# The first column group of a large block kernel, reordered: each weight column serves both token halves in turn, filler matmuls in the gap, filter tables ahead of token rows, Hyena side work 8 tiles later

## The reference, cut to what matters

```python
hn = rmsnorm(x, norm1_w)                       # x: 256 x 2048
proj = hn @ w_in                               # the first product of the kernel
conv_out = centred_depthwise_conv(proj[..., :5120], conv_w, conv_b)
filt = hyena_filters(L, w1, b1, f1, w2, b2, f2, w3)   # two sine layers, then w3
z   = hx1 * long_conv(hv, kf[:, 0], hb[0])
y_a = hx2 * long_conv(z,  kf[:, 1], hb[1])
```

## Time and profile before

| what | value |
|---|---|
| median of 3 runs | 2603.71 us (2602.76 to 2605.73) |
| profiled execution, its own time | 2605.0 us |
| its span | 2603.2 us |
| PE busy | 2592.2 us of the span |
| ACT, POOL, DVE busy | 1407.6, 1208.0, 1129.5 us |
| HBM over the span | 188 GB/s |

### The profile page before, as it was taken

How to read it: one execution, slowest core, us unless ns; L and a number is a source line. 1 busy time by engine, 2 the same in 40 slices (tenths; PEclk the granted TensorE clock), 3 DMA queues, 4 the chain that set the end, 5 groups by cost and what they waited for, 6 DMA issues and landing times.

```text
span 2603.2 us, 30124 instructions
## 1 busy us (share of the span) xinstructions
PE 2592.2 (100%) x11856; PEld 2146.5 (82%) x11856; DVE 1129.5 (43%) x1324; ACT 1407.6 (54%) x1727; POOL 1208.0 (46%) x528
## 2 busy tenths in 40 slices
PE   9999999999999999999999999999999999999999
PEld 7888888788888888888888888888888888888887
DVE  5898955434442232323333466456533232322222
ACT  7677654445565555555544575565555555555333
POOL 2777843344444444444444455333444444444443
PEclk9999999999999999999999999999999999999999
DMA  8776654466666666666666644554566666666554
GB/s 298 220 201 205 193 186 162 147 233 210 202 196 211 204 205 205 205 207 202 209 207 210 212 162 162 173 184 146 178 203 204 208 202 210 202 210 202 202 202 146
DMA packets 174588, 515.84 MB, mean 198 GB/s; under 512 B 108027, under 2 KB 111068, under 8 KB 117104
## 3 DMA queue, kind: packets, MB, share of 16 engines
q1 hardware_dynamic: 174016, 513.40, 61.3%
q10 hardware_dynamic: 432, 0.52, 0.1%
HBM read 487.14 MB, written 2.10 MB: 188 GB/s over the span
## 4 chain that ended last, share of the span: by engine, by line
PE 94%; DVE 2%; DMA 1%; ACT 1%; POOL 1%; issue 1%; SPq 0%; ACTq 0%; DVEq 0%; POOLq 0%
PE PB L735 30%; PE PB L739 30%; PE PB L736 30%; DMA RAW<-in_w_in_a 1%; DVE WL L2011 1%; PE PB L971 1%; PE PB L815 0%; PE PB L933 0%; PE PB L753 0%; PE PB L855 0%; PE PB L845 0%; ACT WH L1256 0%; POOL WL L2967 0%; PE PB L1088 0%; PE PB L1028 0%
## 5 line engine op out<-in xcount | busy, mean ns | idle before, releaser
L2967 POOL TENSOR_TENSOR WL<-RAW,WH 128x1024 fp32r<-128x1024 f32 x441 | 1086.8, 2465 | 1378.0 <-ACT WH L1256 1377.7
L1256 ACT ACTIVATE WH<-RAW 128x1024 fp32r<-128x1024 f32 x889 | 938.8, 1058 | 1070.0 <-PE PB L739 1061.0
L2011 DVE TENSOR_TENSOR WL<-RAW,WH 128x1024 fp32r<-128x1024 f32 x448 | 614.7, 1373 | 1380.9 <-ACT WH L1256 1380.7
L735 PE MATMUL PB<-WH,HNH 128*128 128x512 f32 x2464 | 970.5, 394 | 2.2 <-ACT WH L1544 1.9
L739 PE MATMUL PB<-WL,HNH 128*128 128x512 f32 x2464 | 960.9, 390 | 2.1 <-POOL WL L2967 2.0
L736 PE MATMUL PB<-WH,HNL 128*128 128x512 f32 x2464 | 960.1, 390 | 0.0
L735 PEld LDWEIGHTS PB<-WH,HNH 128*128 128x128 f32 x2464 | 463.2, 188 | 102.2 <-issue 7.4
L739 PEld LDWEIGHTS PB<-WL,HNH 128*128 128x128 f32 x2464 | 463.0, 188 | 102.1 <-POOL WL L2967 4.3
L736 PEld LDWEIGHTS PB<-WH,HNL 128*128 128x128 f32 x2464 | 463.4, 188 | 94.3
L735 PE MATMUL PB<-WH,HDH 128*128 128x512 f32 x704 | 273.9, 389 | 0.0
L736 PE MATMUL PB<-WH,HDL 128*128 128x512 f32 x704 | 273.9, 389 | 0.0
(11 more groups left out here) (376 smaller groups left out, 1926.3 us busy)
## 6 DMA issues: line engine op xcount, KB each, us to landing
RAW<-in_w_gu SPq DMA_DIRECT2D x176, 1024.0 KB, 4.8
RAW<-in_w_dn SPq DMA_DIRECT2D x88, 1024.0 KB, 4.8
RAW<-in_w_in_a SPq DMA_DIRECT2D x53, 1024.0 KB, 5.3
RAW<-in_w_in SPq DMA_DIRECT2D x45, 1024.0 KB, 4.8
RAW<-in_w_out SPq DMA_DIRECT2D x32, 1024.0 KB, 4.8
RAW<-in_w_ga SPq DMA_DIRECT2D x24, 1024.0 KB, 4.7
RAW<-in_w_gb SPq DMA_DIRECT2D x24, 1024.0 KB, 4.8
WIN<-in_win SPq DMA_DIRECT2D x8, 512.0 KB, 6.5
```

Source lines behind the costliest of these rows:

```text
L735: e.matmul(o, hi[:, k, x], WH[:, s, c], start=k == 0, stop=False)
L1256: e.activation(WH[:, u % NSPL, :], RAW[:, n % NRAW, half * SU * 128:(half + 1) * SU * 128], ACT.Copy).then_inc(*wt.act.mark(("wh", u)))
L2011: e.tensor_tensor(WL[:, u % NSPL, :], RAW[:, n % NRAW, half * SU * 128:(half + 1) * SU * 128], f32(WH[:, u % NSPL, :]), ALU.subtract).then ...
L2967: e.tensor_tensor(WL[:, u % NSPL, :], RAW[:, n % NRAW, half * SU * 128:(half + 1) * SU * 128], f32(WH[:, u % NSPL, :]), ALU.subtract).then ...
```

## The change

Eight edits, all in the first part of the kernel:

1. Ahead of group 0, 11 ONES matmuls instead of 9.
2. Group 0 has a function of its own, `first_group`: for each column k it does h = 0 and then h = 1 (six matmuls), and between column 1 and column 2 it runs 7 more ONES matmuls.
3. Unit 1's WH and WL are made in two halves, each behind the token column that it goes with.
4. SP: the filter tables ZT and FW1 go ahead of XTOK, and XTOK's second MB goes behind the next weight transfer.
5. ACT: two squares at units 6 and 7, two at tiles 1 and 3 of group 1. `token_root` moves from tile 1 to tile 14 of group 1, `projected(0)` from tile 4 to 15, the two splits of group 0 from 6 and 9 to 17 and 20, the joins from 42 and 45 to 44 and 47, the middle taps from 46 and 49 to 48 and 51. DVE's part of the root moves to tile 14, behind `low(12)`.
6. SP: the transposes of group 0 move from tile 4 to tile 22 of group 1.
7. PE: the first filter matmul moves from tile 0 to tile 8 of group 1.
8. Hyena begins 8 tiles later on all engines (4.5 instead of 4); some taps of later groups move by 3 to 9 tiles to fit.

```diff
-            for h in range(2):
-                e.dma_start(XTOK[:, h, :], A["x"][:, h, :]).then_inc(landed["xtok"], 16)
-            w.beside(hyena(), 1.8, 4)
-            run(2 * 16)
             e.dma_start(ZT[:, :], A["zt"]).then_inc(landed["zt"], 16)
             e.dma_start(FW1[0:33, 0:64], A["filt_w1"]).then_inc(landed["fw1"], 16)
             e.dma_start(FW1[0:64, 64:192], A["filt_w2"]).then_inc(landed["fw2"], 16)
+            e.dma_start(XTOK[:, 0, :], A["x"][:, 0, :]).then_inc(landed["xtok0"], 16)
+            w.beside(hyena(), 1.8, 4.5)
+            run(16)
+            e.dma_start(XTOK[:, 1, :], A["x"][:, 1, :]).then_inc(landed["xtok1"], 16)
+            run(16)
...
-                if 1 <= g < 11 and k == 4:
+                if 1 <= g < 11 and k == (22 if g == 1 else 4):
                     projected_turned(g - 1)
...
+            def ones(n):
+                for i in range(n):
+                    e.matmul(mb(2)[:, 0:128], ONES[:, :], ONES[:, :], start=True, stop=True)
+
+            def first_group(banks):
+                ready = hn_ready(0)
+                for n in w.tiles(64):
+                    if n % 8:
+                        continue
+                    u = w.i // SU
+                    s = u % NSPL
+                    for r in range(2):
+                        k, c = n // 4 + r, slice(r * 512, (r + 1) * 512)
+                        if k == 2:
+                            ones(7)
+                        ready(k)
+                        for h in range(2):
+                            o, x = banks[h][:, 0:512], slice(h * 128, (h + 1) * 128)
+                            if h == 0 and (r == 0 or u < 2):
+                                e.wait_ge(*wt.act.done("wh", u, *([r] if u < 2 else [])))
+                            e.matmul(o, HNH[:, k, x], WH[:, s, c], start=k == 0, stop=False)
+                            e.matmul(o, HNL[:, k, x], WH[:, s, c], start=False, stop=False)
+                            if h == 0 and (r == 0 or u < 2):
+                                e.wait_ge(*wt.dve.done("wl", u, *([r] if u < 2 else [])))
+                            t = e.matmul(o, HNH[:, k, x], WL[:, s, c], start=False, stop=k == 15)
...
-            for i in range(9):
-                e.matmul(mb(2)[:, 0:128], ONES[:, :], ONES[:, :], start=True, stop=True)
-            w.beside(hyena(), 1.8, 4)
+            ones(11)
+            w.beside(hyena(), 1.8, 4.5)
...
-                    hooks[{3: 36, 6: 32}.get(g, 40)] = lambda: banks_for_taps(g - 1)
+                    hooks[{3: 36, 5: 48, 10: 48}.get(g, 40)] = lambda: banks_for_taps(g - 1)
...
-                    hooks[0] = first_filter_layer
+                    hooks[8] = first_filter_layer
...
+            e.wait_ge(landed["x1"], 16)
+            for k in range(2):
+                r, q = slice(512 * k, 512 * k + 512), slice(1024 + 512 * k, 1536 + 512 * k)
+                normed(0, 2 + k, "norm1", XT[:, 2 + k, :])
+                if k == 0:
+                    e.wait_ge(raw_landed[0], 16)
+                e.activation(WH[:, 1, r], RAW[:, 0, q], ACT.Copy).then_inc(...)
...
-                if k in (6, 9):
-                    projected_split(g, (k - 6) // 3)
-                at = 39 if g == 5 else 42
+                at = 17 if g == 0 else 6
+                if k in (at, at + 3):
+                    projected_split(g, (k - at) // 3)
+                at = 44 if g == 0 else 42
                 if k in (at, at + 3):
                     projected_joined(g, (k - at) // 3)
-                if k in (at + 4, at + 7):
-                    conv_middle(g, (k - at - 4) // 3)
+                at = {0: 48, 4: 51, 9: 51}.get(g, 46)
+                if k in (at, at + 3):
+                    conv_middle(g, (k - at) // 3)
...
-                    if g == 1 and k == 1:
+                    if g == 1 and k in (1, 3):
+                        first_square(2 + k // 2)
+                    if g == 1 and k == 14:
                         e.wait_ge(*m.pool.done("eps"))
                         token_root(0)
-                    if g == 1 and k == 4:
+                    if g == 1 and k == 15:
                         projected(0)
...
-            token_rstd(0)
             e.wait_ge(landed["vec"], 16)
             for g in range(1, 10):
                 for k in tiles(64):
-                    at = 45 if g == 6 else 48
+                    if g == 1 and k == 14:
+                        token_rstd(0)
+                    at = {1: 50, 5: 53}.get(g, 48)
```

More of the change, by code:

```diff
@@ L711, in tile_row @@
                 ntile(mb(nt)[:, 0:T], HNH, HNL, range(n), [("nt", nt)], ready, hooks)
+            def ones(n):
[22 more added lines that the diff above has]
+                            t = e.matmul(o, HNH[:, k, x], WL[:, s, c], start=False, stop=k == 15)
+                            steps = ([("nt", NT["a"] + h)] if k == 15 else []) + ([("unit", u)] if h and r else [])
+                            if steps:
+                                t.then_inc(*wt.pe.mark(*steps))
             def group(nt, hi, lo, K, ready=None, hooks={}, banks=None, part=None, in_turn=False):
@@ L732, in group @@
                             ready(k)
-                        if h == 0 and (r == 0 or u == 0):
-                            e.wait_ge(*wt.act.done("wh", u, *([r] if u == 0 else [])))
+                        if h == 0 and r == 0:
+                            e.wait_ge(*wt.act.done("wh", u))
                         e.matmul(o, hi[:, k, x], WH[:, s, c], start=k == 0, stop=False)
                         e.matmul(o, lo[:, k, x], WH[:, s, c], start=False, stop=False)
-                        if h == 0 and (r == 0 or u == 0):
-                            e.wait_ge(*(wt.dve.done("wl", 0, r) if u == 0 else low_half(u)))
+                        if h == 0 and r == 0:
+                            e.wait_ge(*low_half(u))
                         t = e.matmul(o, hi[:, k, x], WL[:, s, c], start=False, stop=k == K - 1)
@@ L1123, in tensor @@
                     hooks[32] = gates
-                group(NT["a"] + 2 * g, HNH, HNL, 16, None if g else hn_ready(0), hooks, banks)
+                group(NT["a"] + 2 * g, HNH, HNL, 16, None, hooks)
             w.rest()
@@ L1552, in first_square @@
                 h, c = divmod(i, 2)
-                if i == 0:
-                    e.wait_ge(landed["xtok"], 32)
+                if c == 0:
+                    e.wait_ge(landed[f"xtok{h}"], 16)
                 x = XTOK[:, h, 1024 * c:1024 * c + 1024]
                 e.activation(x, x, ACT.Square, accum_out=SSQ[:, 0, h, c:c + 1]).then_inc(*m.act.mark(("sq", 0, i)))
[L1558 to L1561, removed]
+            e.wait_ge(landed["x1"], 16)
[4 more added lines that the diff above has]
+                    e.wait_ge(raw_landed[0], 16)
+                e.activation(WH[:, 1, r], RAW[:, 0, q], ACT.Copy).then_inc(*wt.act.mark(("wh", 1, k), *([("wh", 1)] if k else [])))
+            w.beside(hyena(), 1.8, 4.5)
             def first_steps(u):
@@ L1631, in short_conv @@
             def short_conv(g, k):
-                if k in (6, 9):
-                    projected_split(g, (k - 6) // 3)
-                at = 39 if g == 5 else 42
+                at = 17 if g == 0 else 6
+                if k in (at, at + 3):
+                    projected_split(g, (k - at) // 3)
+                at = 44 if g == 0 else 42
                 if k in (at, at + 3):
                     projected_joined(g, (k - at) // 3)
-                if k in (at + 4, at + 7):
-                    conv_middle(g, (k - at - 4) // 3)
-                if g >= 6 and k in (58, 60):
-                    qk_silu(g, (k - 58) // 2)
+                at = {0: 48, 4: 51, 9: 51}.get(g, 46)
+                if k in (at, at + 3):
+                    conv_middle(g, (k - at) // 3)
+                at = 61 if g == 9 else 58
+                if g >= 6 and k in (at, at + 2):
+                    qk_silu(g, (k - at) // 2)
             for k in tiles(64):
@@ L2603, in vector @@
                     *wt.dve.mark(("wl", 0, k), *([("wl", 0)] if k else [])))
[L2604 to L2607, removed]
+            for k in range(2):
+                r, q = slice(512 * k, 512 * k + 512), slice(1024 + 512 * k, 1536 + 512 * k)
+                normed(0, 2 + k, "norm1", XT[:, 2 + k, :])
+                e.wait_ge(*wt.act.done("wh", 1, k))
+                e.tensor_tensor(WL[:, 1, r], RAW[:, 0, q], f32(WH[:, 1, r]), ALU.subtract).then_inc(
+                    *wt.dve.mark(("wl", 1, k), *([("wl", 1)] if k else [])))
+            w.beside(hyena(), 1.8, 4.5)
             def first_steps(u):
@@ L2650, in vector @@
             for k in tiles(16 * 16):
-                if k in (48, 51):
-                    conv_outer(9, (k - 48) // 3)
+                if k in (53, 56):
+                    conv_outer(9, (k - 53) // 3)
             w.rest()
```

18 lines of the change are left out of this document (8 added, 10 removed).

## The result

The changed kernel takes 2631.18 us (median of 4 runs, 2629.95 to 2633.11) against 2603.37 for the kernel before in the same runs (2602.76 to 2605.73): a ratio of 1.0104 [1.0092, 1.0116], 1% slower. The forecast was 2606.2, in a range that ended at 2609.3. The profiled execution has its own time of 2631.8 and a span of 2630.0, 26.8 more than before.

The account below looks back on a forecast made before the run. PE, busy 2592.2 of 2603.2 us, was taken to bound the kernel. A lag of 3.0 at matmul 200 less 0.5 for Hyena gave +2.5 on the median 2603.7: 2606.2 us, range 2600.5 to 2609.3.

Parts of the forecast that it names:

- The start: First group and loads: matmul 24 at 14.7 against 16.48, matmul 104 at 33.2 against 36.91, a lead of 3.7 us.
- The root behind unit 12: Group 1: the root delays unit 13's low part to 48.8; PE waits 2.7 us at matmul 158, lead 1.4.
- the sine's at 50.9: Second filter matmul, ahead of matmul 162: 1.2 us of waiting for the sine, turning the lead into a lag of 0.5.
- PE being late, ACT and POOL regain their distance: After matmul 200: ACT and POOL regain their distance; only the Hyena shift's 0.5 us gain was counted there.
- the late transposes as far as `high(17)`: Transposes behind transfer 9 delay ACT's joins and unit 17: 2.5 us of waiting, matmul 200 at 62.7, 3.0 behind.
- The Hyena shift: Gap before 82.74 should go: 0.5 us gained, bounds 1.2 of gain and 1.3 of loss.
- The clock did fall again: Rival: one wait at matmul 158 or after puts PE at 1.2 GHz, 2.8 us more: 2609.0; chance 0.12.
- one of the signs that I named: Sign that the prediction is wrong: matmuls lie 0.42 us apart after 46 us.
- The kept lead: Rival: unit 13 ready by 46.1, nothing after it late; 3.5 us gained, up to 4.2: 2600.2 to 2599.5; chance 0.13.
- the filler raised the clock: Start: PE working without a gap raises the clock early; rival without this, matmul 24 at 17.3, still 2606.2, chance 0.05.

Follow-up runs that it names:

- the changed kernel with the swap: The changed kernel, root late, with even units' low parts on POOL and odd ones' on DVE from unit 18 to 111: 2614.49 us, ratio 1.0042.
- The swap: The kernel before with Hyena 8 tiles later, taps moved, and even units' low parts on POOL, odd ones' on DVE, units 18 to 111: 2605.29 us.
- The mirror: The kernel before with even units' low parts on POOL and odd ones' on DVE from unit 18 to 111, Hyena not shifted: 2610.46 us, ratio 1.0028.
- the root put back: The changed kernel with group 0's root and what hangs on it early, and Hyena and all taps as before: 2605.12 us, ratio 1.0004.
- the first-group run: The kernel before with only edits 1 to 3 (11 ONES, first_group with 7 ONES, unit 1 in halves): 2604.44 us, ratio 0.9999.

## Why the prediction was wrong

**The start: right in its time, in part by luck.** Matmul 24 was put at 14.7 and came at 14.23, with the clock up before 10 us. Matmul 104 was put at 33.2 after a rest of waiting and came at 32.37 with none. But the clock was up at 6.5 already, so column 0 took 1.7 us and not 2.5; and column 1, which I said could not begin before 8.70, began at 8.22. The 7 ONES ran from 9.90 up to the next matmul at 11.38, when the clock had long been up: 1.5 us for which no row shows a return. And the start differs from run to run: with the old first group matmul 24 lies between 15.69 and 17.43 in seven traces, with the new one between 13.48 and 14.53 in seven.

**The root behind unit 12: right in kind, and within 1.1 us at its end.** The table load was expected at 42.2, the wait ahead of matmul 158 at 48.8, the sine's at 50.9, matmul 200 at 62.7. The timeline of ACT, changed kernel:

```profile
38.91 1.06 ACT L1287 ACTIVATE WH<-RAW 128x1024 fp32r<-128x1024 f32 x1 [2.31 <-DMA RAW<-in_w_in_a]
41.45 1.28 ACT L1611 ACT_TABLE_LOAD   x1 [1.48 <-DVE MS L2658]
...
43.33 1.27 ACT L1626 ACTIVATE TM<-PB,RTOK 128x512 f32<-128x512 f32 x2 [0.29 <-DVE RTOK L2660]
44.49 1.05 ACT L1287 ACTIVATE WH<-RAW 128x1024 fp32r<-128x1024 f32 x1
...
57.83 2.57 ACT L1642 ACTIVATE TAP<-PRT 128x1024 uint16<-128x1024 uint16 x2 [5.31 <-DMA PRT<-PRP]
```

The transfer landed 0.8 sooner than I had it, everything up to 48.03 lies 0.8 sooner, and the transposes landed 1.1 later than the end that I took. The lag at matmul 200 was forecast as 3.0 and is 4.1.

**"PE being late, ACT and POOL regain their distance": this step failed first.** It put the loss behind matmul 200 at nothing. Between matmuls 200 and 224 another 7.4 us go: a wait of 2.98 and the slow clock around it. The timeline of DVE, with a row of POOL, changed kernel:

```profile
62.28 0.88 DVE L2083 SCALAR_TENSOR_TENSOR PB<-TAP,VEC,PB 128x255 f32<-128x255 f32 x2 [7.09 <-ACT PB L1654]
...
63.98 0.54 DVE L2120 TENSOR_SCALAR HA<-PB,VEC 128x256 f32<-128x256 f32 x1
...
66.80 0.87 DVE L2083 SCALAR_TENSOR_TENSOR PB<-TAP,VEC,PB 128x255 f32<-128x255 f32 x2
...
68.49 1.22 DVE L2048 TENSOR_TENSOR WL<-RAW,WH 128x1024 fp32r<-128x1024 f32 x1
...
69.38 2.54 POOL L3008 TENSOR_TENSOR WL<-RAW,WH 128x1024 fp32r<-128x1024 f32 x1 [5.64 <-ACT WH L1287]
69.74 2.46 DVE L2186 TENSOR_TENSOR HS<-H,HS 64x256 fp32r<-64x256 f32 x1
```

DVE stands 7.09 us for the late middle taps; behind them stand the range reduction of the second sine, two groups of outer taps, a low part, and only then the filters' low half HS, which ends at 72.20. PE wanted it at 69.3 and stood 2.98 us (the row names PRP, which was done at 70.24). HS itself takes 0.42 us in the kernel before and in eleven of the twelve experiments, and 2.46 here: it begins while POOL's low part runs and ends 0.28 behind it, so some 2 of the 2.98 us are DVE held up by POOL. In the changed kernel with the swap, HS takes 0.42 and PE still waits 3.23 ahead of 70.85; so the late chain is enough for a wait of this size. I had followed the late transposes as far as `high(17)` and stopped; the taps behind the same joins have readers too. That the two parts, root and shift, act together is shown by the table: the late root costs 5.9 with Hyena as before and about 10 with Hyena later, swapped or not.

**The Hyena shift, -0.5 with bounds of -1.2 and +1.3: this is the large error.** This term of the sum was mis-sized: it costs 15 to 20 us, more than ten times the bound. I priced the one gap that it removes and took the nearest wait as the largest possible loss. The question to ask was which instructions a side stream stands beside on each engine after the shift, with what slack: it moves 8 tiles against a pattern of period 16. The swap gives back 17 us, so the loss needs the new distances between Hyena and the low parts. The mirror, with the same distances, loses only 7, so they are not enough. What makes the rest stays open: ACT's waits for KSP are 24.2 us in the mirror with little loss, and those for the filter's weights are 6.0 in the run with Hyena later and the units swapped, with 2 us lost and no wait for KSP.

**The rivals.** The clock did fall again, which was also one of the signs that I named, and not once but four times, for 8.6 us in all; I gave this 0.12 and a price of 2.8. Two of the falls (50.9 and 64.6) stand beside waits that I had forecast, the other two beside waits that I had not. The kept lead failed for the root's sake, as argued, but with the root put back it fails too (2605.1), by the chain that starts at 82.8 whatever PE does. That the filler raised the clock is not shown: it was up ahead of the 7 ONES in all seven traces with the new first group, and no run has the new order of columns without the ONES.

## What to carry to other kernels

Before a side stream is shifted, list its instructions on each engine against the period of the main stream's work there, and read the slack of the next buffer handed over (here 0.50 us on an engine that was busy 46% of the time); a shift by half a period meets other neighbours all the way, and can cost far more than any wait now in the trace. A lead gained at the start is only kept if every chain that runs by another engine's clock is brought forward too. The bounds of an edit that touches hundreds of us should not come from the largest single wait of before, but from such a wait times the number of meetings. Here that is 8 blocks times 1.33, 10.6 us: an estimate, and still under the 15 to 20 measured.

## What the runs showed of the hardware

**A short stop can cost the clock, and doesn't always.** In the changed kernel matmuls go from 0.23 to 0.43 us apart at about 50.9, after stops of 1.71 and 1.02 us; around 64.6, after 1.71; inside the stop of 2.98 ahead of 72.30; and at 262.5, in the one of 3.09. They don't after 2.89 us ahead of 226.04, nor after 2.13 ahead of 328.85, nor in the first-group run after 2.00 ahead of 32.61.

The clearest case is one and the same wait, ahead of matmul 734: 2.89 us in the changed kernel and 2.90 with Hyena later, without a fall; 2.79 with the root early, and the clock is down from 215.5. So the length of a stop alone doesn't decide. Before this study I took 1.33 us as the size that does nothing; the stops of 1.11 and 1.30 us at 63.43 and 65.93 in the run with Hyena and later taps back came with a fall at 65.7. At the start, too, the clock can go both ways. With the old first group the clock goes up between 3.8 and 9.4 us in four of seven traces and falls again before it stays up, from 13.5 to 16.2 on; in the other three it goes up once, at 12.8 to 14.0; with the new one it goes up at 3.9 to 6.5 and stays.

The Trainium skill (TensorE: Matmul & The Clock Gate, "What's actually happening") says that idleness brings the throttle back; the falls here agree, with 8.6 us in all. Per us of idle time it is no constant either: from 17 to 430 us, 15.4 us of idle time came with 3.4 us of lost clock in the change with the root early and with 6.8 in Hyena later alone, 21.6 with 8.6 in the changed kernel.

**POOL and VectorE hold each other up.** A low part of 1024 elements a partition takes 2.40 us on POOL in most places, but 2.5 to 3.5 in 340 of 781 places in 14 traces (60 to 430 us). In all 340 an instruction of DVE was running when it began, and in all but two the low part takes what was left of that instruction and 2.2 to 2.3 us more. DVE's next one is held in turn. The timeline of DVE, kernel before, at the place shown above, where POOL's low part runs from 205.10 to 207.95:

```profile
204.57 1.11 DVE L2186 TENSOR_TENSOR Y<-M 128x512 f32<-128x512 f32 x1
...
205.61 3.42 DVE L2011 TENSOR_TENSOR WL<-RAW,WH 128x1024 fp32r<-128x1024 f32 x1
```

Y ends at 205.68, and 2.27 us later POOL is done; DVE's low part, 1.23 us where nothing is in its way, takes 3.42 and ends 1.08 behind POOL's. Not every instruction of DVE does this: behind a running SCALAR_TENSOR_TENSOR of the taps, or one that reads PB (the banks that PE writes), POOL's low part stayed under 2.5 us in 171 of 172 places. So the length of such a step is not a constant in a sum, and a shift changes it. In total there is no more of it in the changed kernel, where POOL and DVE are busy 9.1 and 14.7 us less than before; it bears on a wait of PE at HS, as above.
